# Query columns spread over the blocks, and eight attention units behind the second projection

## The chip, the core and the metric

The kernel runs on one core of a Trainium2 chip, in one launch. The metric is the device time in microseconds (us). TensorE is named PE, VectorE DVE, ScalarE ACT, GpSimd POOL and SyncE SP, as in the profile.

## The reference

One step of a streaming encoder with D = 1024 channels over 2112 tokens (64 of a running stream, 2048 of a new one). Layer A is a gated linear recurrence, layer B sliding-window attention with 16 heads of 64 that share 2 key/value heads; both add to the residual stream. What matters here is layer B:

```
u = rmsnorm(x) @ w_in;  q, gate = split(u)                 # 1024 query and 1024 gate columns
q = rmsnorm(q.reshape(.., 16, 64), q_norm)                 # mean of squares over each head's 64 columns
s = q k / 8, masked to chunks c-2, c-1, c of 64 frames
p = exp(s - m);  o = p @ v / (sum(p) + exp(sink - m))
y = (o * silu(gate)) @ w_out;  x + y
```

All is float32. Products with weights are made of two float32r halves (high and low), three matmuls for each pair of 128-row blocks.

## The kernel before

Tokens lie along the free dimension, channels on the 128 partitions in NB = 8 blocks. Five stages follow each other: projection of layer A (`a1`), recurrence with output projection and keys and values, projection of layer B (`b1`), attention units with the output projection, and a tail of output blocks. Each engine runs a program of its own, written out by hand, with semaphores between them; there is no planner, and the order in the code is the order on each engine.

The projection of layer B runs in PN = 6 turns of PT = 352 tokens, each of 16 slots j. Slots 0 to 7 make the query blocks, slots 8 to 15 the gate blocks. In a slot `project_tensor` issues 24 matmuls of 352 columns (L769) into one of four PSUM banks; `project_vector` multiplies the result by the reciprocal root mean square of the token (L669, the evacuation). After slot 0 PE makes the sum over the partitions of the squares of the next rms norm, a plain float32 matmul (L775, the token sum); ACT takes the root (L535), DVE the reciprocal (L648).

The norm of the queries works block by block. A block holds two whole heads, 64 partitions each. ACT squares it (L543) and, from turn 2 on, rounds it to a high half (L547); POOL makes the low half (L949); two slots later PE sums over each head with the block-diagonal matrix `head_ones`, as two float32r matmuls (L748, L750), in turn 1 as one plain float32 matmul (L744); ACT takes the root (L560), and DVE makes the reciprocal (L628) and the product (L631) in `norm_head`, three slots behind. So each turn has eight head sums, roots and reciprocals. SP stores each block to DRAM (L484), the gates after ACT's Silu (L564).

In the last turn (s = PN) slots from LATE = NB + 2 = 10 on are late: they use bank 7 alone (a slot's matmuls wait for the evacuation of the slot before, L763), have the Silu made of Tanh (L579) and a product (L1879), and behind each slot's matmuls every engine runs one unit of the attention: units 0 to 5 of 66. Units 0 and 1 are tile 0 (64 tokens), then come 8 units for each tile of 256 tokens. In unit u PE issues the scores of u (L1659), the value products of u-2 (L1709, L1713), the transposes of the probabilities of u-1 (L1674, L1677), from unit 12 on one block of the output projection (L1727), and in the first unit of a tile the transposes of V (L1693 to L1696), which wait until ACT has read the transposed probabilities of the unit before (L1936). DVE makes the maximum (L1781 to L1789), the normalisation behind ACT's exponentials (L1925, L1930) and the copies; at the start of a tile it copies parts of V (L1818, L1820), and the second unit before a tile's end it scales the next tile's keys (L1770). The transposes of unit u-1 wait for the normalisation of u-1. `EARLY_UNITS` is 16 - LATE; `run_attention` runs the rest after the projection. SP loads tiles of queries, keys and V at (PN, 14), (PN, 15) and after, and the gates of a tile whole (L1554).

## Time and profile before

| | |
|---|---|
| median of 3 runs (least to most) | 1533.1 us (1531.64 to 1534.43) |
| profiled execution | 1530.83 us, span 1529.0 us |
| PE, weight loads, DVE, ACT, POOL busy | 97%, 93%, 73%, 49%, 19% |
| reciprocals of the heads (L628) | 48 of 2344 ns |
| DMA | 219.32 MB, mean 143 GB/s |
| layer B's projection on PE | 736.7 us to 1147.1 us |

The span is the profiled execution from its first to its last instruction. A matmul's duration in the rows overlaps the next one's, so the price of one is the distance between two starts.

### The profile page before, as it was taken

All of it is one profiled execution on the core that took longest, in us unless ns stands there. A gap on an engine that the chain in (4) does not pass through costs nothing.

```text
span 1529.0 us, 32072 instructions
## 1 busy us (share of the span) xinstructions
PE 1479.7 (97%) x10752; PEld 1419.8 (93%) x10752; DVE 1110.9 (73%) x2246; ACT 754.1 (49%) x1667; POOL 294.3 (19%) x237
## 2 busy tenths in 40 slices
PE   7999999999899999999899999999997999999999
PEld 7999999999899999998899999999985788888888
DVE  7987766856698898897775583855677877777771
ACT  5443332436887777762354453534346444444440
POOL 0011111101444434431531010110201111111110
PEclk9999999999999999999999999999999999999999
DMA  7565655579855555656332211212255344433312
GB/s 239 170 211 196 227 184 201 180 242 331 285 160 156 170 158 161 183 153 214 111 89 60 86 58 57 90 51 89 79 161 129 89 120 120 114 91 93 104 48 78
DMA packets 202707, 219.32 MB, mean 143 GB/s; under 512 B 60496, under 2 KB 189264, under 8 KB 202576
## 3 DMA queue, kind: packets, MB, share of 16 engines
q1 hardware_dynamic: 190448, 208.27, 43.7%
q10 hardware_dynamic: 12128, 9.39, 1.9%
q8 instruction: 71, 1.16, 0.3%
q14 instruction: 60, 0.49, 0.1%
HBM read 132.56 MB, written 85.30 MB: 142 GB/s over the span
## 4 chain that ended last, share of the span: by engine, by line
PE 59%; DVE 6%; issue 4%; ACT 4%; DMA 1%; POOL 0%; SPq 0%; ACTq 0%; DVEq 0%; POOLq 0%
PE s_banks L769 20%; PE bank L1438 11%; PE bank L1727 10%; PE s_banks L1405 5%; PE bank L1421 3%; PE s_banks L1659 3%; ACT m_p L1925 2%; PE bank L1674 2%; PE bank L1709 2%; PE bank L1713 1%; PE bank L769 1%; DVE m_nmax L1781 1%; PE bank L1677 1%; DVE m_p L1803 1%; DMA x_dram<-r_x 1%
## 5 line engine op out<-in xcount | busy, mean ns | idle before, releaser
L1925 ACT ACTIVATE m_p<-s_banks,m_nm 128x192 f32<-128x192 f32 (+2 forms) x264 | 106.1, 414 | 181.8 <-DVE m_nm L1785 181.5
L1727 PE MATMUL bank<-m_y_hi,w_hi_a 128*128 128x256 f32 (+1 forms) x512 | 149.8, 293 | 2.7 <-DVE w_lo_a L889 2.1
L1727 PE MATMUL bank<-m_y_lo,w_hi_a 128*128 128x256 f32 (+1 forms) x512 | 144.9, 283 | 0.0
L1727 PE MATMUL bank<-m_y_hi,w_lo_a 128*128 128x256 f32 (+1 forms) x512 | 144.8, 283 | 0.0
L769 PE MATMUL bank<-a_hi,w_hi_a 128*128 128x352 f32 x384 | 123.7, 322 | 1.2 <-DVE a_out L669 1.1
L769 PE MATMUL bank<-a_hi,w_lo_a 128*128 128x352 f32 x384 | 124.0, 323 | 0.0
L769 PE MATMUL bank<-a_lo,w_hi_a 128*128 128x352 f32 x384 | 123.9, 323 | 0.0
L628 DVE RECIPROCAL b_qstd<-b_qstd 128x352 f32<-128x352 f32 x48 | 112.5, 2344 | 4.9 <-ACT b_qstd L560 3.2
L1982 POOL TENSOR_TENSOR m_y_lo<-m_y,m_y_hi 128x256 fp32r<-128x256 f32 x66 | 48.6, 736 | 343.8 <-DVE m_y_hi L1838 343.8
L769 PE MATMUL s_banks<-b_hi,w_hi_b 128*128 128x352 f32 x336 | 111.7, 332 | 0.0
L1438 PE MATMUL bank<-r_y_hi,w_hi_a 128*128 128x264 f32 x384 | 109.3, 285 | 0.6 <-ACT r_std L1333 0.6
L573 ACT ACTIVATE a_out_hi<-a_out 128x352 fp32r<-128x352 f32 (+1 forms) x48 | 23.9, 498 | 173.0 <-DVE a_out L717 173.0
L1438 PE MATMUL bank<-r_y_lo,w_hi_a 128*128 128x264 f32 x384 | 109.1, 284 | 0.0
L1438 PE MATMUL bank<-r_y_hi,w_lo_a 128*128 128x264 f32 x384 | 108.8, 283 | 0.0
L769 PE MATMUL s_banks<-b_hi,w_hi_a 128*128 128x352 f32 x336 | 108.8, 324 | 0.0
L769 PE MATMUL s_banks<-b_hi,w_lo_a 128*128 128x352 f32 x336 | 108.4, 323 | 0.0
L769 PE MATMUL s_banks<-b_lo,w_hi_a 128*128 128x352 f32 x336 | 108.4, 323 | 0.0
L769 PE MATMUL s_banks<-b_hi,w_lo_b 128*128 128x352 f32 x336 | 108.3, 322 | 0.0
L769 PE MATMUL s_banks<-b_lo,w_hi_b 128*128 128x352 f32 x336 | 108.2, 322 | 0.0
L1727 PEld LDWEIGHTS bank<-m_y_hi,w_hi_a 128*128 128x128 f32 x512 | 96.6, 189 | 4.7 <-DVE w_lo_a L889 3.8
L1727 PEld LDWEIGHTS bank<-m_y_lo,w_hi_a 128*128 128x128 f32 x512 | 96.8, 189 | 0.0
L1727 PEld LDWEIGHTS bank<-m_y_hi,w_lo_a 128*128 128x128 f32 x512 | 96.2, 188 | 0.0
(226 smaller groups left out, 4782.1 us busy)
## 6 DMA issues: line engine op xcount, KB each, us to landing
w_raw_b<-weights_dram SPq DMA_DIRECT2D x26, 512.0 KB, 4.4
w_raw_a<-weights_dram SPq DMA_DIRECT2D x25, 512.0 KB, 4.7
sga_dram<-a_out SPq DMA_DIRECT2D x48, 176.0 KB, 3.0
r_xc_hi<-xc_hi_dram SPq DMA_DIRECT2D x32, 264.0 KB, 3.0
r_xc_lo<-xc_lo_dram SPq DMA_DIRECT2D x32, 264.0 KB, 3.2
r_xc<-xc_dram SPq DMA_DIRECT2D x32, 264.0 KB, 3.9
r_sg<-sga_dram SPq DMA_DIRECT2D x32, 264.0 KB, 3.6
r_x<-xT_dram SPq DMA_DIRECT2D x64, 132.0 KB, 2.1
```

The costliest lines, as they stand in the source:

```text
L573: nc.scalar.activation(m.out_hi[:, q, 0:width], m.out[:, place(m, j), 0:width], ACT.Copy)\
L628: nc.vector.reciprocal(m.qstd[:, :], m.qstd[:, :]).then_inc(m.qrec_done, 1)
L769: mm = nc.tensor.matmul(project_bank(m, s, j)[:, 0:PT], w[pw][:, kt * P:(kt + 1) * P], x[:, kt, :], start=(n == 0), stop=(n == 3 * NB - 1))
L1405: mm = nc.tensor.matmul(bank[2 * mat + ob][:, 0:RT], w[pw][:, at:at + P], x[px][:, q, kt, :].bitcast(F32R), start=(i == 0), stop=(i == 5))
L1421: mm = nc.tensor.matmul(bank[6 + o][:, 0:RT], w[pw][:, blk * P:(blk + 1) * P], (r.x1_hi, r.x1_lo)[px][:, blk % 2, :], start=(blk == 0 and ...
L1438: mm = nc.tensor.matmul(bank[4 + blk % 2][:, 0:RT], w[pw][:, kt * P:(kt + 1) * P], (r.y_hi, r.y_lo)[px][tp][:, kt, :], start=(i == 0), sto ...
L1659: mm = nc.tensor.matmul(s_banks[:, 2 * (i % 2) + e, bp * 192 + v0:(bp + 1) * 192], m.q[par][rows, j, blk:blk + 2, :].rearrange("p b t -> p ...
L1674: nc.tensor.transpose(bank[4][:, k * P:(k + 1) * P], m.p[:, i % 2, k, 0:P], ident[:, :])
L1709: nc.tensor.matmul(bank[6][e * HEAD:(e + 1) * HEAD, 0:AT], m.v[par][:, j, n * HEAD:(n + 1) * HEAD], m.pt_a[:, e * AT:(e + 1) * AT], start= ...
L1727: mm = nc.tensor.matmul(out_bank(ts, blk)[:, 0:width], w[pw][:, kt * P:(kt + 1) * P], (m.y_hi, m.y_lo)[px][tp][:, kt, 0:width], start=(n = ...
L1925: nc.scalar.activation(m.p[:, q, k, v0:192], s_banks[:, 2 * q + e, bp * 192 + v0:(bp + 1) * 192], ACT.Exp, bias=m.nm[:, q, k:k + 1], accum ...
L1982: nc.gpsimd.tensor_tensor(y_part(m.y_lo, s, par, i), m.y[:, q, :, :], y_part(m.y_hi, s, par, i).bitcast(F32), ALU.subtract).then_inc(m.y_l ...
```

## The change

The columns of the query weights are laid out anew on the host: block b holds columns 8p + b for partitions p, so that a partition carries, over the eight blocks, eight columns of one head, and a head lies on eight neighbouring partitions. The store undoes it in its addressing (`"(p b) t -> p b t"`). DVE adds the eight squared blocks up (`add_query`), and one plain float32 matmul behind slot 8 sums over each head's eight partitions with a new matrix, which POOL makes in turn 1 in the place of `head_ones` (`spread_heads`). One root (slot 9) and one reciprocal (`invert_heads`, end of slot 9) serve all eight blocks, whose products follow two by two in slots 10 to 13 (`norm_heads`), and so do their stores. The high and low halves of the squares, and with them POOL's part, are gone. The queries have eight buffers, the outputs two.

LATE is NB = 8 in place of 10, so that slots 8 to 15 of the last turn are late and carry units 0 to 7. The loads of tile 2 and of the gates move with them. Memory is laid out anew around it. The core of the diff:

```diff
+        spread_ones = head_ones
...
+                    m.q2, m.qacc = b(f"{tag}_q2", [P, 2, PT]), b(f"{tag}_qacc", [P, PT])
...
-                m.out = b(f"{tag}_out", [P, 4, PT if heads else PT + HALO])
+                m.out = b(f"{tag}_out", [P, 2 if heads else 4, PT if heads else PT + HALO])
+                if heads:
+                    m.q, m.qstd = b(f"{tag}_q", [P, NB, PT]), b(f"{tag}_qstd", [P, PT])
...
-                last = m.heads and isinstance(s, int) and s == PN
-                for j in ([0, 1, 2, 3, 4, 5, 8, 6, 9, 7] + list(range(10, 2 * NB))) if last else range(2 * NB):
+                for j in range(2 * NB):
...
+                        if m.heads and not gate:
+                            continue
...
+                        if m.heads:
+                            eng.dma_start(dst[:, blk, cols(t * PT, PT)], m.out[:, blk % 2, :])\
+                               .then_inc(m.stored[place(m, j)], 16)
+                            for q in normed_at(j):
+                                eng.wait_ge(m.q_normed, NB * t + q + 1)
+                                eng.dma_start(m.dst[0].rearrange("(p b) t -> p b t", p=P)[:, q, cols(t * PT, PT)], m.q[:, q, :])\
+                                   .then_inc(m.stored[place(m, q)], 16)
+                        elif two_pieces(m, s, gate):
...
-        LATE = NB + 2
+        LATE = NB
...
-                            need(eng, m.qms_done, NB * t + j - 1)
-                            nc.scalar.activation(m.q2[:, j % 2, :], m.q[:, j % 4, :], ACT.Square)\
+                            need(eng, m.q2_added, NB * t + j - 1)
+                            if j == 0 and isinstance(s, int) and s == 1:
+                                eng.wait_ge(r.kms_done, RN)
+                            nc.scalar.activation(m.q2[:, j % 2, :], m.q[:, j, :], ACT.Square)\
                               .then_inc(m.q2_done, 1)
-                            if not (isinstance(s, int) and s == 1):
-                                eng.wait_ge(m.q2_done, NB * t + j + 1)
-                                nc.scalar.activation(m.q2_hi[:, j % 2, :], m.q2[:, j % 2, :], ACT.Copy)\
-                                  .then_inc(m.q2_high, 1)
...
-                        if m.heads and 2 <= j < NB + 2:
-                            q = j - 2
-                            eng.wait_ge(m.qms_done, NB * t + q + 1)
-                            need(eng, m.q_normed, NB * t + q)
-                            nc.scalar.activation(m.qstd[:, :], bank[5 + q % 2][:, 0:PT], ACT.Sqrt,
+                        if m.heads and j == NB + 1:
+                            eng.wait_ge(m.qms_done, t + 1)
+                            need(eng, m.q_normed, NB * t)
+                            nc.scalar.activation(m.qstd[:, :], bank[6][:, 0:PT], ACT.Sqrt,
                                                  scale=1.0 / HEAD, bias=eps[:, 0:1]).then_inc(m.qstd_done, 1)
...
-                        need(eng, m.late_done, j - LATE - 1)
-                        nc.scalar.activation(m.q[:, j % 2, :], m.out[:, place(m, j), 0:PT], ACT.Tanh)\
-                          .then_inc(m.late_tanh, 1)
+                        need(eng, m.late_done, j - LATE)
+                        nc.scalar.activation(m.late_tmp[:, :], out_part(m, j), ACT.Tanh).then_inc(m.late_tanh, 1)
...
-        def norm_head(eng, m, t, q):
-
-            eng.wait_ge(m.qstd_done, NB * t + q + 1)
+        def out_part(m, j):
+
+            return m.out[:, part(m, j)[1] % 2 if m.heads else place(m, j), 0:PT]
+
+        def normed_at(j):
+
+            return range(2 * (j - NB - 2), 2 * (j - NB - 2) + 2) if NB + 2 <= j < NB + 6 else ()
+
+        def add_query(eng, m, t, q):
+
+            eng.wait_ge(m.q2_done, NB * t + q + 1)
+            if q == 0:
+                need(eng, m.qms_done, t)
+                nc.vector.tensor_copy(m.qacc[:, :], m.q2[:, 0, :]).then_inc(m.q2_added, 1)
+            else:
+                eng.wait_ge(m.q2_added, NB * t + q)
+                nc.vector.tensor_tensor(m.qacc[:, :], m.qacc[:, :], m.q2[:, q % 2, :], ALU.add).then_inc(m.q2_added, 1)
+
+        def invert_heads(eng, m, t):
+
+            eng.wait_ge(m.qstd_done, t + 1)
             nc.vector.reciprocal(m.qstd[:, :], m.qstd[:, :]).then_inc(m.qrec_done, 1)
-            eng.wait_ge(m.qrec_done, NB * t + q + 1)
-            need(eng, m.stored[place(m, q)], stored_before(m, t, q))
-            nc.vector.tensor_tensor(m.out[:, place(m, q), :], m.q[:, q % 4, :], m.qstd[:, :], ALU.mult)\
-              .then_inc(m.q_normed, 1)
+
+        def norm_heads(eng, m, t, j):
+
+            for q in normed_at(j):
+                eng.wait_ge(m.qrec_done, t + 1)
+                nc.vector.tensor_tensor(m.q[:, q, :], m.q[:, q, :], m.qstd[:, :], ALU.mult).then_inc(m.q_normed, 1)
...
-                        if m.heads and NB <= j < NB + 3 and not late(m, s, j):
-                            norm_head(eng, m, t, j - 3)
...
-                        if m.heads and 3 <= j < NB:
-                            norm_head(eng, m, t, j - 3)
+                        if m.heads and 1 <= j < NB:
+                            add_query(eng, m, t, j - 1)
                     continue_input(s, par, j)
+                    if known(s, 1, PN) and m.heads:
+                        if j == NB - 1:
+                            add_query(eng, m, t, j)
+                        if j == NB + 1:
+                            invert_heads(eng, m, t)
+                        norm_heads(eng, m, t, j)
...
-            def head_sum(t, q):
-
-                need(eng, m.qstd_done, NB * t + q - 1)
+            def head_sum(t):
+
                 if isinstance(t, int) and t == 0:
-                    eng.wait_ge(m.q2_done, q + 1)
-                    nc.tensor.matmul(bank[5 + q % 2][:, 0:PT], head_ones[:, :], m.q2[:, q % 2, :], start=True, stop=True)\
-                      .then_inc(m.qms_done, 1)
-                    return
-                eng.wait_ge(m.q2_low, NB * (t - 1) + q + 1)
-                nc.tensor.matmul(bank[5 + q % 2][:, 0:PT], head_ones[:, :].bitcast(F32R), m.q2_hi[:, q % 2, :],
-                                 start=True, stop=False)
-                nc.tensor.matmul(bank[5 + q % 2][:, 0:PT], head_ones[:, :].bitcast(F32R), m.q2_lo[:, q % 2, :],
-                                 start=False, stop=True)\
+                    eng.wait_ge(spread_made, 2)
+                eng.wait_ge(m.q2_added, NB * (t + 1))
+                need(eng, m.qstd_done, t)
+                nc.tensor.matmul(bank[6][:, 0:PT], spread_ones[:, :], m.qacc[:, :], start=True, stop=True)\
                   .then_inc(m.qms_done, 1)
...
-                    if m.heads and 2 <= j < NB + 2:
-                        head_sum(t, j - 2)
+                    if m.heads and j == NB:
+                        head_sum(t)
...
+        def spread_heads(eng):
+
+            eng.wait_ge(r.kms_done, RN)
+            spread = spread_ones[:, :].rearrange("p (h c) -> p h c", c=NB)
+            nc.gpsimd.affine_select(out=spread, in_=ones[:, :].rearrange("p (h c) -> p h c", c=NB), compare_op=ALU.is_ge,
+                                    fill=0.0, base=0, pattern=[[-NB, P // NB], [0, NB]], channel_multiplier=1)\
+              .then_inc(spread_made, 1)
+            eng.wait_ge(spread_made, 1)
+            nc.gpsimd.affine_select(out=spread, in_=spread, compare_op=ALU.is_ge, fill=0.0, base=NB - 1,
+                                    pattern=[[NB, P // NB], [0, NB]], channel_multiplier=-1).then_inc(spread_made, 1)
+
         def project_gpsimd(eng, m, after):
             def body(s, par):
-                t = s - 1
                 for j in range(2 * NB):
                     if isinstance(s, int) and s == 1 and j + 2 < 2 * NB:
                         low_part(eng, nc.gpsimd, m.unit + j + 2)
-                    if j < NB and not (isinstance(s, int) and s == 1):
-                        eng.wait_ge(m.q2_high, NB * (t - 1) + j + 1)
-                        nc.gpsimd.tensor_tensor(m.q2_lo[:, j % 2, :], m.q2[:, j % 2, :],
-                                                m.q2_hi[:, j % 2, :].bitcast(F32), ALU.subtract).then_inc(m.q2_low, 1)
+                        if j == 1:
+                            spread_heads(eng)
                     after(s, j)
 
             body(1, 1)
-            with eng.Fori(0, (PN - 2) // 2) as i:
-                body(i * 2 + 2, 0)
-                body(i * 2 + 3, 1)
             body(PN, PN % 2)
...
-                eng.wait_ge(b1.qms_done, NB * PN)
+                eng.wait_ge(b1.qms_done, PN)
...
-                                   (PN, 8): gate_sample, (PN, 11): gate_first, (PN, 14): lambda: tile(2, 0, (0,)),
-                                   (PN, 15): lambda: tile(2, 0, (1,))})
+                                   (PN, 8): gate_sample, (PN, 10): gate_first, (PN, 12): lambda: tile(2, 0, (0,)),
+                                   (PN, 13): lambda: tile(2, 0, (1,)), (PN, 14): lambda: tile(2, 0, (2,)),
+                                   (PN, 15): lambda: tile(2, 0, (3,))})
             load_unit(eng, U_OUT_B + NB - 1, b1.proj_done, 2 * NB * PN)
-            tile(2, 0, (2,))
+            tile_gate(2, 0)
...
-                    eng.wait_ge(b1.qstd_done, NB * PN - 1)
...
-                if isinstance(s, int) and (s, i) == (0, 0):
-                    norm_head(eng, b1, PN - 1, NB - 1)
...
+    in_b = g["w_in_b"][0]
+    queries = in_b[:, :D].reshape(D, P, NB).transpose(0, 2, 1).reshape(D, D)
     weights = np.concatenate([in_a, gates, columns(g["w_kv"]), columns(g["w_out_a"][0]),
-                              columns(g["w_in_b"][0]), columns(g["w_out_b"][0])], 0)
+                              columns(queries), columns(in_b[:, D:]), columns(g["w_out_b"][0])], 0)
```

## Rows read from the trace of the kernel before

**Rows 1.** The page: busy time (share of the span) of each engine
```profile
PE 1479.7 (97%) x10752; PEld 1419.8 (93%) x10752; DVE 1110.9 (73%) x2246; ACT 754.1 (49%) x1667; POOL 294.3 (19%) x237
```

**Rows 2.** Timeline of TensorE (start us, us, engine, line, operation): token sum of turns 2 to 4
```profile
810.07 0.46 PE L775 MATMUL bank<-b_acc,ones 128*128 128x352 f32 x1
...
875.98 0.46 PE L775 MATMUL bank<-b_acc,ones 128*128 128x352 f32 x1
...
940.45 0.46 PE L775 MATMUL bank<-b_acc,ones 128*128 128x352 f32 x1
```

**Rows 3.** Timeline of TensorE: after a token sum, and head sums of two neighbouring slots
```profile
1005.10 0.75 PE L775 MATMUL bank<-b_acc,ones 128*128 128x352 f32 x2
...
1005.85 0.32 PE L769 MATMUL s_banks<-b_lo,w_hi_b 128*128 128x352 f32 x1
...
1094.56 0.32 PE L748 MATMUL bank<-b_q_hi,head_ones 128*128 128x352 f32 x1
...
1098.71 0.32 PE L748 MATMUL bank<-b_q_hi,head_ones 128*128 128x352 f32 x1
```

**Rows 4.** Timeline of TensorE: the one wait for GpSimd at a head sum
```profile
819.54 0.43 PE L748 MATMUL bank<-b_q_hi,head_ones 128*128 128x352 f32 x1 [0.99 <-POOL b_q_lo L949]
```

**Rows 5.** Head sums of turn 1 by line (ns least/median/most, first and last start)
```profile
L744 PE MATMUL bank<-b_q,head_ones x16: 457/459/564, 751.5 to 782.9; 128*128 128x352 f32 x16
```

**Rows 6.** A group of the page (busy, mean ns), and GpSimd's select by line
```profile
L628 DVE RECIPROCAL b_qstd<-b_qstd 128x352 f32<-128x352 f32 x48 | 112.5, 2344 | 4.9 <-ACT b_qstd L560 3.2
L2014 POOL TENSOR_SCALAR_AFFINE_SELECT ident<-ident x1: 292/292/292, 1.2 to 1.2; 128x128 f32<-128x128 f32 x1
```

**Rows 7.** Timeline of TensorE: the slots that carry attention units
```profile
1111.30 0.93 PE L1659 MATMUL s_banks<-m_k,m_q 64*128 64x192 f32 x8
...
1119.38 0.30 PE L1674 MATMUL bank<-ident,m_p 128*128 128x128 f32 x1 [1.87 <-DVE m_v_last L1820]
...
1134.52 0.45 PE L1659 MATMUL s_banks<-m_k,m_q 64*128 64x64 f32 x4
...
1147.10 0.39 PE L1659 MATMUL s_banks<-m_k,m_q 64*128 64x128 f32 x2
```

**Rows 8.** Windows: busy us of PE, PEld, DVE, ACT, POOL, granted clock, DMA share, GB/s
```profile
1120.60:1126.20 5.60, 5.57 (x24) 5.38 (x24) 3.21 (x9) 2.69 (x11) 0.00 (x0) 0.70 0.93 287
1130.70:1134.50 3.80, 3.80 (x25) 3.60 (x23) 1.41 (x4) 1.85 (x4) 0.00 (x0) 1.00 0.11 39
```

**Rows 9.** Timeline of TensorE: attention units behind the projection
```profile
1157.67 0.60 PE L1659 MATMUL s_banks<-m_k,m_q 64*128 64x192 f32 x4
...
1162.12 0.44 PE L1659 MATMUL s_banks<-m_k,m_q 64*128 64x192 f32 x2
...
1174.34 0.33 PE L1693 MATMUL bank<-ident,m_vt 128*128 128x128 f32 x1 [2.52 <-ACT m_pt_a L1936]
...
1179.40 0.44 PE L1659 MATMUL s_banks<-m_k,m_q 64*128 64x192 f32 x2
```

**Rows 10.** Timeline of VectorE in those slots
```profile
1113.28 0.17 DVE L1785 TENSOR_TENSOR m_nm<-m_nmax,neg_sink 128x4 f32<-128x4 f32 x1
...
1119.98 0.51 DVE L669 TENSOR_TENSOR b_out<-bank,b_std 128x352 f32<-128x352 f32 x1
...
1124.85 0.52 DVE L1879 SCALAR_TENSOR_TENSOR b_out<-b_q,b_out 128x352 f32<-128x352 f32 x1
...
1126.37 0.52 DVE L669 TENSOR_TENSOR b_out<-bank,b_std 128x352 f32<-128x352 f32 x1 [1.00 <-issue]
```

**Rows 11.** Timeline of ScalarE in those slots
```profile
1113.96 1.28 ACT L1925 ACT_TABLE_LOAD   x1
...
1115.26 0.42 ACT L1925 ACTIVATE m_p<-s_banks,m_nm 128x192 f32<-128x192 f32 x1
...
1121.58 0.42 ACT L1925 ACTIVATE m_p<-s_banks,m_nm 128x192 f32<-128x192 f32 x1 [3.96 <-DVE m_nm L1785]
...
1129.21 0.60 ACT L1936 ACTIVATE m_pt_a<-bank 128x512 f32<-128x512 f32 x1
```

More of the change, by code:

```diff
@@ L139, in build @@
         const_pool = sem("const_pool")
+        spread_made = sem("spread_made")
         lw_step = sem("lw_step")
@@ L172, in project_memory @@
                 if heads:
-                    m.sq, m.acc, m.std = b(f"{tag}_sq", [P, 1, PT]), b(f"{tag}_acc", [P, 1, PT]), b(f"{tag}_std", [P, PT])
+                    m.sq = b(f"{tag}_sq", [P, 1, PT])
+                    with ExitStack() as raw:
+                        m.acc = tensors(raw)(f"{tag}_acc", [P, 1, PT])
+                    b(f"{tag}_gap", [P, 32])
+                    m.late_tmp = b(f"{tag}_late_tmp", [P, PT])
+                    m.std = b(f"{tag}_std", [P, PT])
                 if not heads:
@@ L215, in project_memory @@
                 m.late_tanh, m.late_done = sem(f"{tag}_late_tanh"), sem(f"{tag}_late_done")
-                m.q2_done, m.q2_high, m.q2_low = (sem(f"{tag}_q2_{k}") for k in ("done", "high", "low"))
+                m.q2_done, m.q2_added = sem(f"{tag}_q2_done"), sem(f"{tag}_q2_added")
                 m.qms_done = sem(f"{tag}_qms_done")
@@ L226, in project_memory @@
             m.x_loaded = sems(f"{tag}_x_loaded", 4 if heads else NB)
-            m.stored = sems(f"{tag}_stored", m.out.shape[1])
+            m.stored = sems(f"{tag}_stored", 4)
             return m
@@ L477, in body @@
                         dst = m.dst[gate].rearrange("(b p) t -> p b t", p=P)
-                        if two_pieces(m, s, gate):
+                        if m.heads:
[6 more added lines that the diff above has]
+                        elif two_pieces(m, s, gate):
                             eng.dma_start(dst[:, blk, 0:SAMPLE], m.out[:, place(m, j), 0:SAMPLE])\
@@ L563, in body @@
                             eng.wait_ge(m.evacuated, 2 * NB * t + j + 1)
-                            nc.scalar.activation(m.out[:, place(m, j), 0:PT], m.out[:, place(m, j), 0:PT], ACT.Silu)\
-                              .then_inc(m.silu_done, 1)
+                            nc.scalar.activation(out_part(m, j), out_part(m, j), ACT.Silu).then_inc(m.silu_done, 1)
                     unit = project_unit(m, s, j)
@@ L659, in body @@
                             need(eng, m.stored[place(m, j)], stored_before(m, t, j))
-                            dst = m.out[:, place(m, j), 0:PT]
+                            dst = out_part(m, j)
                         elif m.heads:
-                            dst = m.q[:, j % 4, :]
+                            dst = m.q[:, j, :]
                         else:
@@ L667, in body @@
                         if m.heads and j < NB:
-                            need(eng, m.q_normed, NB * t + j - 3)
+                            need(eng, m.stored[place(m, j)], 16 * (NB // 2) * t)
                         nc.vector.tensor_tensor(dst, project_bank(m, s, j)[:, 0:PT], m.std[:, :], ALU.mult)\
@@ L1706, in values @@
                 if isinstance(s, int) and (s, i) == (0, 0):
-                    eng.wait_ge(b1.qstd_done, NB * PN)
+                    eng.wait_ge(b1.qstd_done, PN)
                 for e in range(2):
@@ L1877, in after_project @@
                     eng.wait_ge(b1.late_tanh, j - LATE + 1)
-                    gate = b1.out[:, place(b1, j), 0:PT]
-                    nc.vector.scalar_tensor_tensor(out=gate, in0=b1.q[:, j % 2, :], scalar=1.0, in1=gate, op0=ALU.add,
+                    gate = out_part(b1, j)
+                    nc.vector.scalar_tensor_tensor(out=gate, in0=b1.late_tmp[:, :], scalar=1.0, in1=gate, op0=ALU.add,
                                                    op1=ALU.mult).then_inc(b1.late_done, 1)
```

13 lines of the change are left out of this document (2 added, 11 removed).

## The prediction

> **What bounds the kernel now.** The page comes first: PE is busy for 1479.7 of 1529.0 us, DVE for 73%, ACT for half, POOL for a fifth [rows 1]. So an edit pays if it takes time from PE, or fills one of the few stretches where PE waits. The reader then wants PE's timeline in the projection of layer B. The token sums mark the turns: 65.91 us from turn 2 to 3, 64.47 us from turn 3 to 4 [rows 2]. A slot of a query block is 4.15 us from one head sum to the next [rows 3]; it holds 24 matmuls of the projection and the two of the head sum, so a matmul is 0.160 us, the 24 are 3.83 us and the pair is 0.32 us. A plain float32 sum costs more: 0.75 us from the token sum to the second matmul behind it [rows 3], less the one of 0.16 between them, so 0.59 us. Sixteen slots (61.3), eight pairs (2.56) and the token sum (0.59) make 64.45 us, which is turn 3: there PE waits for nothing, and DVE's eight reciprocals of 2.34 us [rows 6] are hidden. Turn 2 is 1.44 us longer, and its one wait is 0.99 us for POOL's low half [rows 4].
>
> Last the stretch in which attention begins. Slot 8 of the last turn starts 0.32 us after 1098.71, at 1099.03 [rows 3]; the scores of unit 0 stand behind slot 10 at 1111.30, those of unit 3 at 1134.52, those of unit 5, behind slot 15, at 1147.10 [rows 7], and those of unit 12, the first unit with output matmuls, at 1179.40 [rows 9]. From unit 3 on a slot with its unit takes 6.29 us (12.58 over two [rows 7]); behind the projection a unit takes 4.45 us [rows 9], with PE waiting in each. In the first three units PE waits too: 1.87 us at the transposes of unit 0 [rows 7], after which the granted clock of the next slot is 0.70 and its 24 matmuls take 5.57 us in place of 3.83 [rows 8], a fall from 2.4 to 1.2 GHz for a part of it, worth 1.7 us. These 80.37 us from 1099.03 to 1179.40 are what the second half of the change rearranges.
>
> **The change part by part.**
>
> **Fewer head sums.** Turn 1 has eight plain float32 sums, sixteen records of L744 [rows 5]; one stays: 7 x 0.59 = 4.1 us. Turns 2 to 5 each lose 8 x 0.32 and get one of 0.59: 1.97 us each, 7.9 us. The wait for POOL in turn 2 goes with the halves: 1.4 us. In the last turn six pairs stand ahead of slot 8: 1.9 us. Together **15.3 us**, all of it on PE, which sets these turns.
>
> **What is added beside it** I cost at nothing on the path. DVE gives up seven reciprocals, 16.4 us a turn, and gets eight adds or copies of 352 columns at some 0.5 us (the evacuation is of that size [rows 10]); it is the reciprocals' room that covers them. The new sum waits for the eighth add, which follows slot 7 by an evacuation, a square, an add and the work on the next input that is queued between, some 3 us, while slot 8 covers 3.8 us. The margin is thin where an input lands late; no row shows this wait, so its bounds are 0 and, if the chain came 1 us late in five turns, 5 us. I take 0, for the next block's load is issued three slots ahead and no longer stands behind the queries' stores on SP. POOL's two selects are 0.29 us each [rows 6] and wait for the last key sum; the weight halves that POOL makes behind them are some slots ahead of PE. On SP the stores of the queries move to slots 10 to 13, two behind each gate store; SP waits there for DVE's products, and behind it stand only stores and the loads of the last turn.
>
> **The units move two slots forward.** Start at T, the start of slot 8. PE: slot 8 is 3.83 and the head sum 0.59, so the scores of unit 0 are at T+4.4 (before: 12.3). From here the path is not PE's but the chain DVE-ACT-DVE, and it is longer than before:
> - scores to the end of the small minimum on DVE: 2.15 us (1111.30 [rows 7] to 1113.45 [rows 10]): T+6.6.
> - table load for Exp, 1.28 us [rows 11]: T+7.9. Exponentials, normalisation, copies of V, key scaling and gate product of slot 8, up to the evacuation of slot 9: 4.72 us (1115.26 [rows 11] to 1119.98 [rows 10]): T+12.6.
> - evacuation to the exponentials of unit 1, 1.60 us (1119.98 to 1121.58). New here: the one root sits on ACT ahead of them in slot 9, so ACT has the root's table and loads Exp's again, after the wait: 1.28 us more. T+15.5. Before, unit 1 had no load.
> - exponentials to the end of the gate product, 3.79 us (1121.58 to 1125.37 [rows 10, 11]): T+19.3.
> - new on this path: `invert_heads`, 2.34 us [rows 6]. Queued behind it on DVE are the evacuation of slot 10 and the maximum of unit 2: T+21.6.
> - evacuation to the end of ACT's copy of the transposed probabilities of unit 1: 3.44 us (1126.37 [rows 10] to 1129.81 [rows 11]): T+25.1. PE waits for that copy at the transposes of V in unit 2, and has by then been done since about T+20: a wait of **some 5 us**.
> - from that copy's end to the scores of unit 3, a slot on: 4.71 us (1129.81 to 1134.52). After a wait that long I expect the lower clock, as after 1.87 us of it before [rows 7, 8], and take the same 1.7 us: T+31.5.
>
> Then PE sets the pace again: four slots of 6.29 us, and 0.2 us as unit 6 is the first in a slot with the full 192 columns: scores of unit 7 at T+56.9. DVE has two products of some 0.5 us more in slots 11 to 13; from evacuation to gate product its slot is 5.39 us (1119.98 to 1125.37 [rows 10]), so 6.4 us with them against PE's 6.29, and less as these units have fewer columns: just hidden. From the last late unit to unit 12 it was 32.30 us (1147.10 to 1179.40); two units of 4.45 go, and 0.5 us comes for the wider last unit: 23.9. In it stays the wait of 2.52 us at tile 2's transposes [rows 9]. Sum: **T+80.8 against 80.4 before**. So the two moved units win 8.9 us behind the projection, the two slots that carry them get 4.9 us longer (6.29 less 3.83 each), and the start-up chain, with reciprocal, second table load and clock, takes the rest. Bounds for this stretch: 5 us better (the wait doesn't come), 5 us worse (below).
>
> Here a page of the Trainium skill speaks against the change: ScalarE: Activation LUTs, section What ACT_TABLE_LOAD costs, says a switch of function set costs its load and a drain of about 1.38 us. The rows don't agree: the load at 1113.96 lasts 1.28 us and the exponential starts at 1115.26 [rows 11]. By the page the two loads on the chain would add 2.8 us, an estimate; the sum goes by the rows.
>
> **The sum.** Minus 15.3 plus 0.4 is minus 14.9 us. The profiled execution took 1530.83 us (its span and 1.8 us around it), so 1516.0 us; it lies 2.3 us under the median of the runs shown, and against that median, 1533.1 us, the time is **1518.3 us**.
>
> **The rivals.**
> - **The overlap works.** ACT or DVE get through the first units without the wait of 5 us, say because the sums above double a step. The stretch is then 5 us better: 1513. For it: two of the steps are from a slot at the lower clock. Against: every step waits for the one before.
> - **The late slots are DVE's.** The 6.4 us of DVE in slots 11 to 13 exceed PE's 6.29, PE waits a little in each, the clock falls once or twice more at 1.7 us, and a head sum waits here and there: 5 us worse, 1523.
> - **The drain counts.** The skill's page named above is right where ACT changes sets between waits: as this kernel's chain runs through two loads, 2.8 us are added: 1521. The rows show no such drain.
> - **The head sum waits in every turn.** Eight squares and adds in one chain end later than slot 8; at 2.5 us in six turns it gives 15 us back: 1533, no change. It needs a chain of 6.3 us where I count 3.
> - **Slower.** The clock stays at 1.2 GHz through the late slots, because each has a gap now: the 24 matmuls of a slot then take twice 3.83 us, 3.8 us more, over eight slots 31 us: 1549. It decides from four slots on, where the 14.9 us are used up. Against: the slots from unit 3 on are back at PE's pace, at a granted clock of 1.00 just ahead of unit 3 [rows 8].
>
> **How the numbers follow.** Forecast 0.64 (its own range 1515.5 to 1521), overlap works 0.11, late slots DVE's 0.13, drain 0.02, head sum waits 0.06, slower 0.04. Two runs of this kernel can be told apart from 0.2%, 3.1 us. Faster by more than that are the first four cases: 0.90; within it 0.06; slower 0.04. The range 1512.5 to 1523.5 takes in the first four but their edges and leaves out the last two.
>
> **What would show it right or wrong.** In the profile after: token sums 62.5 us apart from turn 2 to 3 on, and POOL without work there; no wait of PE at the head sum; scores of unit 0 4.4 us after slot 8's start; a wait of some 5 us at the transposes of V in unit 2, with a lower clock behind it; slots of 6.3 us from unit 3 on; 24 us from the scores of unit 7 to those of unit 12. Turns that stay at 64.5 us would make the first half wrong; a start-up without the long wait, or late slots above 6.6 us, the second.

## The result, and the profile after

The changed kernel takes 1519.5 us (median of four runs, 1518.58 to 1520.08) beside 1532.4 us for the kernel before (1531.45 to 1534.43), a ratio of 0.991 with an interval of 0.990 to 0.993: 12.8 us less. Its profiled execution took 1520.08 us, with a span of 1518.3 us, 10.7 less than the span before. The profiled execution before lay 1.5 us under that median and this one 0.5 us over its own, so the traces explain 10.7 us and the medians have 2.1 more. Its page, beside [rows 1]:

```profile
PE 1469.9 (97%) x10668; PEld 1409.0 (93%) x10668; DVE 1042.4 (69%) x2254; ACT 709.0 (47%) x1584; POOL 258.1 (17%) x199
```

Its lines are renumbered: the token sum is L797 (before L775), the head sum L773, the evacuation L691 (L669), the big reciprocal L650 (L628), the scores L1687 (L1659; L1686 and L1688 in some experiments), the values L1736, the transposes of V L1720 (L1693), ACT's exponentials L1950 (L1925), its copy of the transposed probabilities L1961 (L1936).

**The turns**, TensorE's timeline (columns as in [rows 2]): three token sums, the head sum between, and VectorE's last add ahead of it.

```profile
806.14 0.75 PE L797 MATMUL bank<-b_acc,ones 128*128 128x352 f32 x2
...
836.58 0.52 DVE L645 TENSOR_TENSOR b_qacc<-b_qacc,b_q 128x352 f32<-128x352 f32 x1
837.63 0.76 PE L773 MATMUL bank<-b_qacc,head_ones 128*128 128x352 f32 x2
...
868.99 0.75 PE L797 MATMUL bank<-b_acc,ones 128*128 128x352 f32 x2
...
931.83 0.75 PE L797 MATMUL bank<-b_acc,ones 128*128 128x352 f32 x2
```

A turn is 62.85 us, the same from turn 2 to turn 5, where [rows 2] had 65.91 and 64.47. The head sum has no wait in brackets in any turn; the eighth add ends at 837.10, 0.5 us ahead of it.

**The start of attention**, TensorE: scores of units 0, 3, 4 and 7, the transposes of V of units 2 and 10, scores of unit 12; to be laid beside [rows 7, 9].

```profile
1089.71 0.93 PE L1687 MATMUL s_banks<-m_k,m_q 64*128 64x192 f32 x8
...
1107.82 1.12 PE L1720 MATMUL bank<-ident,m_vt 128*128 128x128 f32 x4 [4.06 <-ACT m_pt_a L1961]
1113.91 0.67 PE L1687 MATMUL s_banks<-m_k,m_q 64*128 64x64 f32 x8
1120.19 0.72 PE L1687 MATMUL s_banks<-m_k,m_q 64*128 64x128 f32 x8
...
1139.37 0.93 PE L1687 MATMUL s_banks<-m_k,m_q 64*128 64x192 f32 x8
...
1158.19 0.66 PE L1720 MATMUL bank<-ident,m_vt 128*128 128x128 f32 x4 [2.52 <-ACT m_pt_a L1961]
...
1163.26 0.93 PE L1687 MATMUL s_banks<-m_k,m_q 64*128 64x192 f32 x8
```

The wait of 4.06 us is the start-up chain's. The windows on either side of it (columns as in [rows 8]) show PE nearly idle and then at a granted clock of 0.71, the fall that followed a wait in [rows 8] too:

```profile
1103.00:1108.00 5.00, 0.94 (x7) 0.71 (x8) 4.45 (x12) 1.87 (x10) 0.72 (x1) 0.95 0.94 283
1108.00:1113.00 5.00, 5.00 (x25) 4.96 (x25) 2.93 (x7) 1.85 (x4) 0.00 (x0) 0.71 0.23 90
```

**One thing that nobody forecast.** Unit 12's scores are 16.1 us earlier than before (1163.26 against 1179.40 of [rows 9]), yet the end is only 10.7 us earlier. The tiles of 256 tokens show where: from tile 3 on it is 44.5 to 45.6 us from the V transposes of one tile to those of the next, the same in both kernels, except from tile 5 to tile 6, where it was 46.96 us (1312.73 to 1359.69) and now is 51.20 (1297.12 to 1348.32). Tiles 4 and 5 are the first pass of the hardware loop over tiles, tiles 6 and 7 the second, so this is where the loop jumps back. TensorE's timeline there, the kernel before:

```profile
1354.27 0.93 PE L1659 MATMUL s_banks<-m_k,m_q 64*128 64x192 f32 x8 [1.66 <-issue]
```

and the changed kernel, its timeline and then two windows of 2 and 3 us:

```profile
1338.65 0.93 PE L1687 MATMUL s_banks<-m_k,m_q 64*128 64x192 f32 x8 [1.64 <-issue]
1342.08 0.58 PE L1736 MATMUL bank<-m_pt_a,m_v 128*64 128x256 f32 x1 [1.55 <-issue]
```

```profile
1340.00:1342.00 2.00, 0.53 (x3) 0.00 (x0) 1.28 (x3) 0.57 (x3) 0.00 (x0) 0.50 0.01 4
1342.00:1345.00 3.00, 2.92 (x17) 2.59 (x16) 0.72 (x2) 1.24 (x7) 0.44 (x1) 0.50 0.03 5
```

"issue" is time in which PE waited for no engine and no load of data that the profile shows.
### The profile page after: what moved, and what is told of

It is laid out like the page before. It is cut to its first block, busy times and chain, and to the rows that moved or that the text cites. A ratio compares the mean times of both kernels' runs of the same rounds, so it can differ in the third digit from the quotient of the medians.

```text
span 1518.3 us, 31662 instructions
## 1 busy us (share of the span) xinstructions
PE 1469.9 (97%) x10668; PEld 1409.0 (93%) x10668; DVE 1042.4 (69%) x2254; ACT 709.0 (47%) x1584; POOL 258.1 (17%) x199
## 4 chain that ended last, share of the span: by engine, by line
PE 62%; DVE 5%; ACT 2%; issue 2%; DMA 1%; SPq 0%; ACTq 0%; POOL 0%; DVEq 0%
PE s_banks L791 22%; PE bank L1754 10%; PE bank L1465 10%; PE s_banks L1432 5%; PE s_banks L1687 3%; PE bank L1448 3%; PE bank L791 2%; PE bank L1702 2%; PE bank L1736 2%; ACT m_p L1950 2%; PE bank L1740 1%; DVE m_nmax L1808 1%; PE bank L1705 1%; DMA r_x<-xT_dram 1%; DMA x_dram<-r_x 1%
## 5 line engine op out<-in xcount | busy, mean ns | idle before, releaser
L1950 ACT ACTIVATE m_p<-s_banks,m_nm 128x192 f32<-128x192 f32 (+2 forms) x264 | 106.1, 414 | 185.8 <-DVE m_nm L1812 185.5
L578 ACT ACTIVATE a_out_hi<-a_out 128x352 fp32r<-128x352 f32 (+1 forms) x48 | 23.9, 498 | 172.8 <-DVE a_out L745 172.8
L791 PE MATMUL s_banks<-b_hi,w_hi_a 128*128 128x352 f32 x320 | 104.1, 325 | 0.0
L791 PE MATMUL s_banks<-b_hi,w_lo_a 128*128 128x352 f32 x320 | 103.3, 323 | 0.0
L791 PE MATMUL s_banks<-b_lo,w_hi_a 128*128 128x352 f32 x320 | 103.2, 323 | 0.0
L791 PE MATMUL bank<-a_hi,w_hi_b 128*128 128x352 f32 x288 | 93.3, 324 | 0.3 <-DVE a_out L691 0.3
```

Of the source, the lines that this page charges most:

```text
L578: nc.scalar.activation(m.out_hi[:, q, 0:width], m.out[:, place(m, j), 0:width], ACT.Copy)\
L791: mm = nc.tensor.matmul(project_bank(m, s, j)[:, 0:PT], w[pw][:, kt * P:(kt + 1) * P], x[:, kt, :], start=(n == 0), stop=(n == 3 * NB - 1))
L1950: nc.scalar.activation(m.p[:, q, k, v0:192], s_banks[:, 2 * q + e, bp * 192 + v0:(bp + 1) * 192], ACT.Exp, bias=m.nm[:, q, k:k + 1], accum ...
```

## The experiments

The theory was the prediction's own sum, with two sizes off and one loss outside it. What had to be told apart: how much each half of the change gives; whether the reciprocal in the chain is what PE waits for; and whether the second stop belongs to what the change does or only to where it puts the code.

**The first half alone.** The queries spread, but late slots from 10 on and the loads where they were:

```diff
-        LATE = NB
+        LATE = NB + 2
```

> The spread queries alone: eight late units go back to six (LATE = NB + 2, the loads of tile 2 and of the gates where they were), all else as in the changed kernel. My theory: turns of 62.85 us, as with the change, so about 13.9 us less than before up to slot 8 of the last turn. In the late slots the reciprocal in slot 9 is out of the chain of units 0 to 2, so the stretch from slot 8 to unit 12 comes out near before, 80.4 us, less 0.2 to 2 us. If no gap in PE's instruction stream falls behind the attention loop: 1518 us, as fast as the whole change or faster. Rival: the two moved units are worth the 4 us that their slots promise (two units of 4.45 us behind the projection against 2.46 us each in it); then this kernel is 4 us slower than the changed one, 1523 to 1524 us.

Measured: 1523.7 us (1521.37 to 1524.28) beside 1532.3; ratio 0.994 [0.993, 0.996]. That is the time of the rival, but not by its reason, as the trace shows. The scores of unit 0 come at 1099.06, 12.2 us earlier than in [rows 7], and from there to the first output matmul it is 71.14 us against 71.16 before: the attention's start is untouched. The end of the recurrence came 2.1 us later in this profile (more on that below); without that the first half is worth 14.3 us at this point. The jump back costs here as in the changed kernel: 51.75 us from tile 5 to 6, with stops of 1.67 and 2.25 us. So the loss at the loop is there without the moved units. From the start of slot 8 to the first output matmul the changed kernel takes 81.5 us, this one and the kernel before 83.4: moving the units wins 1.9 us by itself, not 4. Of the 4.2 us between the two medians the profiles put 1.7 on the end of the recurrence and some 0.5 on the jump back, which the units have nothing to do with.

**The reciprocal out of the chain.** `invert_heads` a slot later and the products in slots 11 to 14:

```diff
-            return range(2 * (j - NB - 2), 2 * (j - NB - 2) + 2) if NB + 2 <= j < NB + 6 else ()
+            return range(2 * (j - NB - 3), 2 * (j - NB - 3) + 2) if NB + 3 <= j < NB + 7 else ()
...
-                        if j == NB + 1:
+                        if j == NB + 2:
                             invert_heads(eng, m, t)
```

> The changed kernel with the one reciprocal of a turn a slot later, at the end of slot 10, and the eight products in slots 11 to 14. My theory: in the last turn the reciprocal stood in the chain from unit 1 to the transposes of V in unit 2; without it PE waits there 4.06 - 2.34 = 1.7 us in place of 4.06, and the clock behind it falls for a shorter time or not at all: 2.3 to 4 us less than the changed kernel, 1515.5 to 1517 us. Slot 14, whose unit has the full 192 columns, has two more products on DVE and may get 0.3 us longer. Rival: the chain has other members of the same length (ACT's root and table load), so that the wait stays near 4 us and the time near 1519.5.

Measured: 1517.2 us (1515.87 to 1518.82), just above the theory's range; ratio 0.991 [0.989, 0.993]. Timeline of PE and DVE:

```profile
1105.23 0.66 PE L1720 MATMUL bank<-ident,m_vt 128*128 128x128 f32 x4 [1.86 <-ACT m_pt_a L1961]
...
1108.50 2.35 DVE L650 RECIPROCAL b_qstd<-b_qstd 128x352 f32<-128x352 f32 x1
1109.88 0.67 PE L1687 MATMUL s_banks<-m_k,m_q 64*128 64x64 f32 x8
```

The wait falls from 4.06 to 1.86 us, by 2.20 where the reciprocal takes 2.35, and from the scores of unit 0 (1089.31) to those of unit 3 it is 20.57 us in place of 24.20. The 3.6 us are more than the wait: the matmuls behind it are faster too (the transposes take 0.66 where they took 1.12). The reciprocal in its new place runs beside the slot's matmuls and holds nobody up.

**Is it the code's place?** A semaphore addition on PE that nobody waits for moves the code behind it and changes nothing that is computed. First 48 of them where PE waits anyway, ahead of the V transposes of unit 2:

```diff
+                if isinstance(s, int) and (s, i) == (1, 0):
+                    for _ in range(48):
+                        nc.tensor.sem_inc(spare, 1)
```

> The changed kernel with 48 instructions more in PE's program (additions to a semaphore that nobody waits for), put ahead of the transposes of V of unit 2, where PE waits 4.06 us anyway. Nothing that is computed changes; every instruction of PE behind them lies 48 places further on. My theory: the 4.3 us that the changed kernel loses behind the attention loop (a gap of 1.55 us that cuts a group of four value products in two, and the lower clock behind it) is PE waiting for its own instructions, and depends on where they lie; with another place the gap goes or moves, and the time is 3.5 to 4.5 us less, about 1515.5 us. Rival: the gap comes of data, a transfer or a semaphore; then it stays where it is and the time is 1519.5 us, or 1521 if the 48 instructions cost something.

Measured: 1517.7 us (1516.67 to 1519.91); ratio 0.991 [0.989, 0.992]. Both stops at the jump are gone and the stretch from tile 5 to 6 is 46.34 us in place of 51.20. The time is less than the expectation's rival and 2.2 us above its theory. The additions, taken for free, are not: they take longer than the wait that should hide them.

```profile
1111.71 1.08 PE L1721 MATMUL bank<-ident,m_vt 128*128 128x128 f32 x4 [5.77 <-issue]
```

5.77 us over 48 is 0.12 us for one. With the reciprocal late as well, where the wait is only 1.86 us, that should cost all of what it gives:

> Both edits, the later reciprocal and the 48 instructions. If both theories hold the gains add up: 6 to 8 us less than the changed kernel, 1512 to 1513.5 us. If the 48 instructions, with less of a wait to hide in, cost their own time, 1514.

Measured: 1519.9 us (1518.01 to 1522.07); ratio 0.992 [0.991, 0.994]; 46.97 us at the jump, but 26.7 us from the scores of unit 0 to those of unit 3. Cover gone, gain gone, and neither of the two expected times came. So the additions went to the front, ahead of PE's first matmul, which waits for the first load and VectorE until about 10 us anyway:

```diff
+            for _ in range(48):
+                nc.tensor.sem_inc(spare, 1)
             recurrent_tensor(eng)
```

> The changed kernel with the same 48 instructions ahead of PE's first matmul, where it waits some 10 us for data (they took 5.8 us in the run before this one, so they should cost nothing here). All code of PE lies 48 places on, as it did at the attention loop in e2. My theory: both gaps at the exit of the attention loop go (1.64 and 1.55 us), the turn of eight units over the exit takes 46.3 us in place of 51.2, and the time is 4.5 to 5 us less than the changed kernel, 1514.5 to 1515. A gap at another loop's exit may come or go by 1 to 2 us, since those loops are moved too. Rival: e2 lost its gaps through the delay ahead and not through the place of the code; then the gaps are back and the time is 1519.5.

Measured: 1518.1 us (1516.94 to 1519.44) beside 1531.3; ratio 0.992 [0.990, 0.993].

> The later reciprocal and the 48 instructions ahead of the first matmul. The later reciprocal showed 24.2 to 20.6 us from the scores of unit 0 to those of unit 3; with the exit at 46.3 us as well: 1511 to 1512.5 us. If the two don't add up (the later reciprocal only shifts the wait behind it), 1514.5 as e5.

Measured: 1515.5 us (1515.17 to 1516.11); ratio 0.990 [0.988, 0.992], the best of all (its runs all lie below the changed kernel's, though the two ratios, each against runs of before on its own chip, overlap). The first matmul isn't late (9.5 us), and the jump costs 46.88 and 46.72 us. What stands there now, in the first of the two:

```profile
1346.36 0.65 PE L1721 MATMUL bank<-ident,m_vt 128*128 128x128 f32 x4 [1.48 <-ACT m_pt_a L1962]
```

That wait begins on VectorE, which now stops itself at its first operation behind the jump, with the scores done by 1340.2:

```profile
1342.56 0.96 DVE L1809 TENSOR_REDUCE m_nmax<-s_banks 128x4 f32<-128x768 f32 x1 [2.73 <-issue]
```

The same stop of 2.6 to 2.8 us stands in all four kernels with 48 additions. So the jump isn't free there either: the stretch is still 1 to 1.7 us over the 45.3 us of the tile ahead of it.

Both are some 3 us slower than expected. The traces say where: compared with the changed kernel the first of them gains 4.3 us at the jump, but it comes to layer B's projection 2.0 us later, and 1.8 of these arise at the end of the recurrence. There stand VectorE's wait and the window behind it, of the changed kernel

```profile
695.87 0.43 DVE L1224 TENSOR_TENSOR r_x<-bank,r_x 128x264 f32<-128x264 f32 x1 [2.06 <-DMA r_x<-xT_dram]
```

```profile
699.00:706.00 7.00, 6.08 (x46) 5.67 (x47) 4.81 (x9) 1.43 (x2) 0.29 (x1) 1.00 0.60 174
```

and of the one with 48 additions at the start:

```profile
697.03 0.43 DVE L1225 TENSOR_TENSOR r_x<-bank,r_x 128x264 f32<-128x264 f32 x1 [3.00 <-DMA r_x<-xT_dram]
```

```profile
699.00:706.00 7.00, 6.33 (x38) 5.61 (x36) 3.96 (x10) 0.29 (x1) 1.43 (x1) 0.76 0.52 158
```

A load lands about 1 us later, PE gets a longer gap, and the clock falls to 0.76. In the profiles of before, of the changed kernel and of the late reciprocal the last two recurrence steps are 39.0 us apart; in all the other experiments it is 40.2 to 42.1 us. With one profile of each it stays open whether this hangs on the code's place too or comes and goes by itself. The four runs of the late reciprocal lie in two pairs, 1515.9 and 1516.0, 1518.5 and 1518.8, and the profiled one, with the short end, is of the lower pair, which hints at the second. Between the profiles of before and after it makes no difference.

**The converse.** If only the place counts, the kernel before should get the second stop when its code is moved. With 116 additions at the start, so many that they can't hide:

> The kernel before with 116 instructions ahead of PE's first matmul (some 14 us, of which the start hides 8 to 10, so it is about 5 us slower for them at the start; what counts is the exit of the attention loop). By my count of PE's instructions the change takes away about 140 ahead of that exit, which is 116 more where places repeat every 256. My theory: the kernel before then shows the changed kernel's two gaps there, and the turn over the exit takes near 51 us in place of 46.96. If my count is off by more than some 20 the second gap lies elsewhere or is not seen. Rival: the gap belongs to the change; then 46.96 stays.

Measured: 1551.3 us, one run. The additions delay the first matmul by 9.7 us, where some 5 were expected, and smaller delays follow in the stages behind. The jump back:

```profile
1368.11 0.93 PE L1660 MATMUL s_banks<-m_k,m_q 64*128 64x192 f32 x8 [1.45 <-issue]
...
1372.10 1.12 PE L1714 MATMUL bank<-m_pt_b,m_v_last 128*64 128x128 f32 x8 [2.47 <-issue]
```

The stretch is 52.07 us in place of 46.96. The second stop, absent before, is there: the old computation with moved code pays the 5 us as well.

**How it hangs on the count.** The changed kernel with 24, 12 and 96 additions at the start. (These expectations call the place the loop's end; it is where the second pass begins.)

> The changed kernel with 24 semaphore additions on TensorE ahead of its first matmul, in place of the 48 that took the two stops of TensorE away where the unit loop ends. Theory, that the stops hang on where the code of the units behind the loop lies: with half the shift both stops may stay, move, or only one go, so the turn from one V transposes to the next across the loop's end lies between 46.9 us (no stop) and 51.2 us (two), and the second stop, if there is one, sits at another instruction than after three value products. Rival, that any addition removes them: 46.9 us whatever the count. The rest of the kernel as it is.

> The same with 12 additions. Theory of place: the turn is 51.2 us or near it, the second stop a dozen instructions earlier in the program than in the changed kernel (that is among the scores, or gone together with the first). Rival: 46.9 us.

> The same with 96 additions. If the stops repeat with the distance that the code is moved, they are back (51 to 52 us, as the kernel before showed with 116 additions: 52.07 us); if 48 were enough for any larger count too, the turn is 46.9 us. The start costs up to 12 us more, as 116 additions put the first matmul 9.7 us later.

The stops, with 12, with 24 and with 96:

```profile
1340.34 0.93 PE L1688 MATMUL s_banks<-m_k,m_q 64*128 64x192 f32 x8 [1.46 <-issue]
...
1344.40 1.12 PE L1737 MATMUL bank<-m_pt_a,m_v 128*64 128x256 f32 x4 [3.13 <-issue]
```

```profile
1339.86 0.82 PE L1688 MATMUL s_banks<-m_k,m_q 64*128 64x192 f32 x2 [1.84 <-issue]
...
1343.42 1.65 PE L1688 MATMUL s_banks<-m_k,m_q 64*128 64x192 f32 x6 [2.74 <-issue]
```

```profile
1348.69 0.93 PE L1688 MATMUL s_banks<-m_k,m_q 64*128 64x192 f32 x8 [2.09 <-issue]
```

| additions ahead | tile 5 to 6 (us) | second stop |
|---|---|---|
| 0 | 51.20 | at the last of the four value records, 1.55 |
| 12 | 51.88 | at the first of them, 3.13 |
| 24 | 52.31 | behind the second of the eight score records, 2.74 |
| 48 | 46.88 | none (nor the first) |
| 96 | 47.38 | none (the first is 2.09) |

(The times of the three, one run each, are 1523.3, 1521.5 and 1526.6 us; at 96 the additions no longer hide, the first matmul is at 16.4 us.) "Any addition removes them" is wrong. "A shift of 12 puts the stop a dozen instructions earlier" is near: it moves from the last value record to the first (five wait instructions stand ahead of that one, and count too), and twelve more move it into the scores. At 24 the stretch is 1.1 us above the range that was expected. At 96 neither case came: the first stop is there, the second isn't. So the stop sits at a place in the program's memory, not at an operation.

**What PE waits for.** The DMA view of the profile lists two queues of kind "instruction", q8 with transfers of 16 KB and q14 with transfers of 8 KB. Over the whole run q8 carries 71 transfers in the changed kernel and in its kernels with 12, 24 and 96 additions, and 62 in all four with 48. As additions to PE's program alone change q8's count, and q14 stays at 64, q8 is read as bringing PE's instructions. The nine that are missing are those of the loop's second pass. From 1330 to 1425 us (queue, kind: transfers, MB, share of the 16 engines), the changed kernel and the one with 48 additions at the start:

```profile
q8 instruction: 9, 0.15, 0.6%
q14 instruction: 5, 0.04, 0.1%
```

```profile
q14 instruction: 5, 0.04, 0.1%
```

With 48 additions PE makes the second pass without a transfer of q8, and without a stop. In the other kernels q8 transfers start shortly ahead of each stop's end: in the changed kernel at 1335.9 us (PE goes on at 1338.65) and at 1339.8 us (1342.08; a third, at 1343.6 us, goes with no stop), in the kernel before at 1351.5 us (1354.27), with 24 additions at 1340.9 us (1343.42). So the stops are PE waiting for its own instructions, which it has to fetch anew for the second pass unless they are all still there. Why 48 places are enough for that and 96 are not (where the loop lies against the 16 KB pieces, presumably) is not shown. The converse fits: the kernel before has 71 transfers, and 90 with its 116 additions. The 19 more fall mostly into two earlier loops, nine each, which ran without any, and one turn of layer A's projection is 1.6 us longer there.

**Two waits.** The table load for Exp ran ahead of the wait on the scores (below). To see whether the number of waits decides, ACT got a second one, long satisfied, ahead of the exponentials of units 0 and 1:

```diff
+                if isinstance(s, int) and s == 0:
+                    eng.wait_ge(b1.ms_done, PN)
```

> The changed kernel with a second wait (on a count reached long before) ahead of the exponentials of units 0 and 1. In the trace of the changed kernel ACT loads Exp's table before the minimum of DVE has come, at 1086.51 and 1096.13, where the forecast had both loads behind it. My theory: with a single wait the load runs ahead of it, since that wait is the exponential's own; with two, one stands ahead of the load. Then both loads are on the chain: the wait of PE at the transposes of V in unit 2 grows from 4.06 to some 6.6 us, and the time by 2.5 us, to 1522. Rival: the load is early for another reason, and nothing moves: 4.06 us, 1519.5.

Measured: 1521.4 us (1519.72 to 1522.79); ratio 0.993 [0.992, 0.995]. The loads stay ahead:

```profile
1087.80 1.28 ACT L1952 ACT_TABLE_LOAD   x1
...
1093.18 0.42 ACT L1952 ACTIVATE m_p<-s_banks,m_nm 128x192 f32<-128x192 f32 x1 [4.09 <-DVE m_nm L1812]
```

and the scores of units 0 and 3 are 24.35 us apart, as in the changed kernel (24.20). The wait at the transposes of V in unit 2 is 4.07 us. The idea fell; most of the median's 1.9 us more is the 1.3 us that the recurrence ended later in this profile. What lets a load ahead is open: elsewhere in the same programs a load does stand behind its wait, as the root's at 876.84 us in the kernel before, which starts after 3.42 us of waiting for PE.

## Why the prediction was right, and where its sizes were off

The time, 1519.5, is in the range and 1.2 us above the forecast; the direction was given 0.90. Two terms were off and one was missing. In the profiles, which the sum was made from, the gain is 10.7 us and not 14.9: head sums 1.4 less, the start-up chain 2.7 more, 4.2 lost at the jump and 1.2 in small delays. Errors of both signs partly cancel there. That the median is nearer still is luck: the medians happen to lie 2.1 us further apart than the profiles, and the median before came out at 1532.4 instead of 1533.1.

- **Head sums.** Forecast 15.3 us by the start of slot 8 in the last turn. It starts at 1085.18 against 1099.03: 13.9 us. Turn 1 gave 4.33 for 4.1. Turn 2 gave 3.06 for 1.97 + 1.4. Turns 3 to 5 gave 1.63, 1.80 and 1.62 where 1.97 each was forecast, and the last turn 1.81 for 1.9; 0.4 was lost ahead. The mis-sized term is the pair: turn 3 gave 1.63 us for eight pairs less one plain sum of 0.59, so a pair was worth 0.28 and not 0.32. The slots are longer than forecast instead: a turn less its two plain sums is 62.85 - 1.18 = 61.67, so a slot is 3.854 us and not 3.83. A forecast turn of 62.5 was 62.85 for the same reason.
- **Added work on DVE and ACT at nothing.** Right: no head sum waits. The margin was 0.5 us (837.10 to 837.63), not the 0.8 that 3.8 less 3 had left.
- **GpSimd.** Its selects took 0.40 us each, not 0.29 [rows 6], hidden as forecast.
- **The start-up chain.** From slot 8's start T, the scores of unit 0 at T+4.5 (4.4), unit 3 at T+28.7 (31.5), unit 7 at T+54.2 (56.9), unit 12 at T+78.1 (80.8). It is 2.7 us shorter, and 2.5 of that lie ahead of unit 1's exponentials (T+13.0 where T+15.5 was forecast). ScalarE's timeline:

```profile
1086.51 1.28 ACT L1950 ACT_TABLE_LOAD   x1
1091.88 0.42 ACT L1950 ACTIVATE m_p<-s_banks,m_nm 128x192 f32<-128x192 f32 x1 [4.09 <-DVE m_nm L1812]
...
1094.26 1.28 ACT L566 ACT_TABLE_LOAD   x1
1095.56 0.56 ACT L566 ACTIVATE b_qstd<-bank,eps 128x352 f32<-128x352 f32 x1
1096.13 1.28 ACT L1950 ACT_TABLE_LOAD   x1
1098.21 0.42 ACT L1950 ACTIVATE m_p<-s_banks,m_nm 128x192 f32<-128x192 f32 x1 [0.79 <-DVE m_nm L1812]
...
1107.16 0.60 ACT L1961 ACTIVATE m_pt_a<-bank 128x512 f32<-128x512 f32 x1
```

  The sum put both Exp loads behind the wait for DVE's minimum. They run ahead of it, while ACT has nothing else to do: 2 x 1.28 us off the chain. In [rows 11] the load did stand directly ahead of the exponentials, but because ACT had just finished a Silu, not because it waits for what the exponentials wait for. The step of the sum that failed is reading a load's place in a busy stretch as its place in the order.
- **The reciprocal and what follows it.** Right in place and size: 2.34 us at 1102.12, the experiment took 2.2 us off the wait. Forecast wait some 5 us, measured 4.06; from the end of ACT's copy to the scores of unit 3 it is 6.15 us (4.71 + 1.7 forecast), the clock at 0.71 as before.
- **The late slots.** Right: 6.3 us each and 25.5 us from unit 3 to unit 7 (25.4), then 23.9 us to unit 12 (23.9), with 2.52 us at tile 2's transposes, the same as in [rows 9].
- **The second half as a whole.** Forecast 0.4 us worse (T+80.8 against 80.4); it is 2.3 us better (T+78.1), by the loads. Counted to the first output matmul it is the 1.9 us of the first experiment.
- **Missing.** The second stop at the jump back, 4.2 us, and small delays behind unit 12 of some 1.2 us. No rival named it: the code after the diff was taken to run as before, as if its place in the program were nothing. Without it the kernel would have been at about 1515, between the forecast and the case "the overlap works".

Of the rivals, "the overlap works" is what happened in part: 2.7 of its 5 us, for another reason than doubled steps. "Late slots DVE's" didn't come: DVE keeps up in slots 11 to 13. "The drain counts" is refuted: the root's load at 1094.26 ends at 1095.54 and the root starts at 1095.56, 0.02 us later, on a switch of function set between two units' exponentials. The Trainium skill (ScalarE: Activation LUTs, What ACT_TABLE_LOAD costs) gives 1.38 us of drain besides; the trace doesn't agree. "Head sum waits" and "slower" didn't come; where the clock did fall it was back within a slot.

## What to carry to other kernels

Cost a step that moves by what its engine does at the new place: an ACT table load was free where it ran while ACT was idle, and a 2.3 us reciprocal between an engine and its next input cost its whole length, until it was moved one slot on. When a change adds or removes instructions ahead of a long loop, look at the first matmuls after the loop jumps back: where there is a stop inside a group, with "issue" as its cause, compare the instruction queues of the DMA view over that pass. Instructions put ahead of the kernel's first matmul can move the stop or take it away, and only a run tells which. Compare the pitch of equal turns or tiles of both traces before explaining a total; here it found 4 us that were in no sum of operations.

## What the runs showed of the hardware that was not expected

- PE can stop after a loop jumps back, 1.5 to 3.1 us, also in the middle of a group of matmuls. Behind the second of two such stops the granted clock was 0.50 (with 0, 12 and 24 additions); behind a single one it was 1.00 (the kernel before, and 96 additions). The place moved with the count of instructions ahead, and the same stretch took 46.3 to 52.3 us.
- The DMA view shows the cause: with the stops the instruction queue q8 carried nine transfers of 16 KB in the loop's second pass, without them none.
- VectorE stopped at the same jump, 2.6 to 2.8 us, visible where PE did not.
- A semaphore addition on PE took 0.12 us (5.77 us for 48).
- An ACT table load (1.28 us) went ahead of a wait that its activation had, with one wait and with two; at 876.84 us in the kernel before another stood behind its wait.
- One plain 128 x 352 float32 sum a turn in place of eight float32r pairs cost PE 0.59 us and no wait: a turn is 62.85 us where it was 64.47.
- At the end of the recurrence a load that landed 1 us later went with 1.8 us more, and a granted clock of 0.76 in place of 1.00 (one pair of profiles).
